# A fused two-model transformer block in fp32 on one core: where the norm factor is applied, which engine adds row sums, and how the decay exponents and the final norm are ordered

## The chip, the cores and the metric

The kernel runs on one core of a Trainium2 chip. TensorE multiplies matrices, VectorE (DVE) and ScalarE (ACT) work on tiles, GpSimd (POOL) does a third share of the elementwise work, and SyncE (SP) issues the DMAs. The metric is the device time of one execution in microseconds; lower is better.

## The reference

The input is 256 tokens of 1024 channels. A first block computes chunked attention, a gated linear recurrence, a merge of the two and a gated feed-forward; its final norm feeds a second block of two layers. Cut to what the change touches:

```python
h = h + (g_a * ya + g_b * yb) @ w_o[l]
hn = rmsnorm(h, norm_ffn_g[l])
g, up = jnp.split(hn @ w_ffn_in[l], 2, axis=-1)
h = h + (jax.nn.silu(g) * up) @ w_ffn_out[l]
return rmsnorm(h, final_norm_g)
...
proj = rmsnorm(h, g) @ w_in                       # gated delta net
qkv = silu(causal_depthwise_conv_2(proj[..., :3 * DN_DIM], conv_w))
gc = cumsum(g); decay = exp(where(tri, gc[:, None] - gc[None, :], -inf))
a_low = where(tri_strict, (k_beta @ k.T) * decay, 0)    # then a triangular solve
...
h = h + square(relu(rmsnorm(h, g) @ w_up)) @ w_down     # mlp, once per layer
return rmsnorm(h, final_norm_g_2)
```

`rmsnorm(x, g)` is x times a factor r of its token (one over the root of the mean square) times g. All of it is float32.

## The kernel before

**Tiling.** The state `H` holds channels on partitions and tokens along the free axis: 8 blocks of 128 channels by 256 tokens. Weights come from HBM in 171 chunks of 128x2048 (1 MB), one at a time through three slots (`RAW`). ScalarE rounds each chunk to fp32r (`WH`, `split_hi`, line 365), VectorE takes the remainder (`WL`, `split_lo`, line 374), and TensorE multiplies in three products: high by high, high by low, low by high (`product`, lines 378 to 380). One chunk makes one step of TensorE: 48 matmuls in `multiply` and `multiply_rows`, 32 in `multiply_wide` (lines 434 and 436). Each step of each engine is written as a body over `st`, and `steps` runs the bodies in a loop of three steps, with a head and a tail unrolled. `split_hi(st)` and `split_lo(st)` work two chunks ahead. All order is written out by hand with semaphores; every engine runs its own program in order.

**Segments**, in order: `xr`, `qk`, `v`, `gr`, `gab`, `ao`, `ro`, `wo`, the feed-forward `fi` (22 chunks) and `fo` (11), then `dq` (12) and `dz` (4), the delta rule without weights, `do`, the first mlp `u0` and `w0` (16 each), `mq`, `mv`, `mo`, the second mlp `u1` and `w1`, and the final norm.

**Norms.** `norm_high` scales two blocks of `H` by the norm's weight and rounds them to `XH` (line 523), and squares them into `XN` (line 516); `norm_low` makes `XL` (line 531). The token's factor r is computed beside the products: POOL adds the squares (`norm_add`), TensorE sums over channels (`norm_sums`), ScalarE takes the root (`norm_root`), VectorE the reciprocal, TensorE turns it into rows (`norm_rows`), and `norm_scale` copies these to `RSTD`. `SUMS_AT` and `ROWS_AT` say after which half step TensorE does its two parts. The output of a projection is multiplied by `RSTD` where it is read out.

**Feed-forward.** In `fi`, ScalarE copies the low half of a step out (`low_half`, line 992), VectorE adds the high half (`add_halves`, line 997), multiplies the gate side by r, and multiplies the two sides after the silu. The up side is not multiplied; r is applied to the output of `fo`. In `u0` and `u1` VectorE computes relu(s) * s (line 1675) on the unscaled s, ScalarE rounds it to `HH` (line 975), VectorE takes `HL` (line 984); r * r is applied to the output of `w0` and `w1`. At the end of `fo`, `w0` and `w1` (`row_chunks`), the last step of TensorE ends one pair of blocks after another. For each pair, VectorE multiplies by `RSTD` into `XN` (`scale_rows`, line 629) and POOL adds that to `H` (`add_rows`, line 642); then ScalarE's `norm_high` and VectorE's `norm_low` prepare the next product, whose first step waits for them pair by pair.

**Delta stage.** During `dq`, VectorE reads each step out into `UQ` (`read_out`, line 1334) and does two taps of the convolution (line 1500); ScalarE does the first tap (line 1163) and POOL the last (`last_tap`, lines 930 and 933). `exponents(g)` builds four heads' decay exponents: two subtractions from rows that TensorE made of `GC` (`decay_rows`), lines 1544 and 1545, and two with `GC` per row, lines 1547 and 1549. `decay_rows(g)` for g of 2 and 3 waits until `exponents(g - 2)` has read its bank. In ScalarE's `dq`, two waits stand ahead of `split_hi`:

```python
if st.i is not None or st.j >= 1:
    act.wait_ge(freed[slot_of(st, -1)], st.uses(-1))
if st.i is not None or st.j >= 3:
    act.wait_ge(s_.tapped, st.local(-3))
split_hi(act, st)
```

**The end.** After `w1` TensorE sums the squares of all 8 blocks over channels with a matrix of ones, so that each partition gets the sum of each token (line 553); ScalarE takes the root of 128x256 (line 574), VectorE the reciprocal of 128x256 (line 1705) and eight products with `H` (line 1709), and SP writes four DMAs.

## Time and profile before

| | us |
|---|---|
| median of 3 runs | 1164.03 (1163.46 to 1165.88) |
| the profiled execution, its own time | 1162.69 |
| its span in the trace | 1161.0 |
| TensorE busy | 1126.1 (97%) |
| VectorE busy | 767.9 (66%) |
| ScalarE busy | 575.7 (50%) |
| POOL busy | 213.3 (18%) |
| mean granted TensorE clock, of full speed | 0.995 |

The span is the time from the first to the last instruction in the trace. A matmul's end is modelled, so neighbouring matmuls overlap in the records; gaps between them are real. "Idle before" is the time in which the engine had nothing to run, with the instruction whose end released it. The chain that ended last is TensorE for 84% of the span and VectorE for 9%.

### The profile page before, as it was taken

What the parts mean: (1) busy time and instruction counts of PE and PEld (TensorE: products, weight loads), DVE (VectorE), ACT (ScalarE), POOL (GpSimd) and SP (SyncE); (2) the same over time, 40 slices, a digit from 0 to 9 for tenths busy, and PEclk for the clock granted to TensorE, in tenths of its full rate; (3) what the DMA queues carried; (4) which work ended last, traced back from release to release, by engine and by line L of the source; (5) the groups of instructions that cost most, each with busy time, mean ns of one, the idle gap of its engine ahead of it and who ended that gap; (6) DMA issues with size and microseconds to landing.
All of it is one profiled execution on the core that took longest, in us unless ns stands there. A gap on an engine that the chain in (4) does not pass through costs nothing.

```text
span 1161.0 us, 21202 instructions
## 1 busy us (share of the span) xinstructions
PE 1126.1 (97%) x8548; PEld 1074.3 (93%) x8548; DVE 767.9 (66%) x944; ACT 575.7 (50%) x749; POOL 213.3 (18%) x222
## 2 busy tenths in 40 slices
PE   6999999999999999998999999999989999999997
PEld 6999889999888999998999888899989999889996
DVE  6647975676877744689896777754467657776333
ACT  6446557445555533565834555543344446554331
POOL 1995003302000001155561010000030002000001
PEclk9999999999999999999999999999999999999999
DMA  9574443645655554345500256655535545655531
GB/s 303 182 232 148 143 138 103 228 158 174 213 186 181 181 210 153 110 146 175 181 8 2 77 178 192 201 188 181 181 115 182 167 140 177 196 186 183 182 142 37
DMA packets 154947, 187.32 MB, mean 161 GB/s; under 512 B 6496, under 2 KB 143872, under 8 KB 154880
## 3 DMA queue, kind: packets, MB, share of 16 engines
q1 hardware_dynamic: 151312, 184.06, 48.5%
q10 hardware_dynamic: 3568, 2.31, 0.7%
q8 instruction: 49, 0.80, 0.3%
q14 instruction: 18, 0.15, 0.0%
HBM read 185.29 MB, written 1.07 MB: 161 GB/s over the span
## 4 chain that ended last, share of the span: by engine, by line
PE 84%; DVE 9%; issue 2%; ACT 2%; DMA 1%; SPq 0%; POOL 0%; DVEq 0%; POOLq 0%; ACTq 0%
PE PS L434 17%; PE PS L378 16%; PE PS L379 16%; PE PS L380 16%; PE PS L436 9%; DVE WL L374 2%; ACT WH L365 1%; DVE XHL L531 1%; PE PS L1892 1%; PE PS L1878 1%; PE PS L723 1%; PE PS L1819 1%; PE PS L1751 1%; DVE QKV L1500 1%; DMA RAW<-in_w_in 1%
## 5 line engine op out<-in xcount | busy, mean ns | idle before, releaser
L374 DVE TENSOR_TENSOR WL<-RAW,WH 128x2048 fp32r<-128x2048 f32 x171 | 405.2, 2370 | 221.5 <-ACT WH L365 221.4
L365 ACT ACTIVATE WH<-RAW 128x2048 fp32r<-128x2048 f32 x171 | 326.8, 1912 | 238.6 <-PE PS L380 196.1
L434 PE MATMUL PS<-XHL,WH 128*128 128x512 f32 x864 | 300.9, 395 | 0.0
L378 PE MATMUL PS<-XHL,WH 128*128 128x256 f32 x832 | 242.5, 291 | 14.9 <-DVE WL L327 6.6
L436 PE MATMUL PS<-XHL,WL 128*128 128x256 f32 x864 | 239.6, 277 | 0.0
L379 PE MATMUL PS<-XHL,WH 128*128 128x256 f32 x832 | 237.1, 285 | 0.0
L380 PE MATMUL PS<-XHL,WL 128*128 128x256 f32 x832 | 236.9, 285 | 0.0
L434 PEld LDWEIGHTS PS<-XHL,WH 128*128 128x128 f32 x864 | 162.1, 188 | 37.5
L378 PE MATMUL PS<-HH,WH 128*128 (+1 forms) x688 | 194.7, 283 | 0.0
L380 PE MATMUL PS<-HH,WL 128*128 (+1 forms) x688 | 194.7, 283 | 0.0
L379 PE MATMUL PS<-HL,WH 128*128 (+1 forms) x688 | 194.7, 283 | 0.0
L378 PEld LDWEIGHTS PS<-XHL,WH 128*128 128x128 f32 x832 | 161.3, 194 | 20.0 <-DVE XHL L531 10.5
L436 PEld LDWEIGHTS PS<-XHL,WL 128*128 128x128 f32 x864 | 162.3, 188 | 0.0
L379 PEld LDWEIGHTS PS<-XHL,WH 128*128 128x128 f32 x832 | 161.3, 194 | 0.3
L380 PEld LDWEIGHTS PS<-XHL,WL 128*128 128x128 f32 x832 | 161.2, 194 | 0.0
L378 PEld LDWEIGHTS PS<-HH,WH 128*128 128x128 f32 x688 | 132.1, 192 | 0.1
L379 PEld LDWEIGHTS PS<-HL,WH 128*128 128x128 f32 x688 | 132.1, 192 | 0.0
L380 PEld LDWEIGHTS PS<-HH,WL 128*128 128x128 f32 x688 | 132.1, 192 | 0.0
L642 POOL TENSOR_TENSOR H<-H,XN 128x512 f32<-128x512 f32 x12 | 15.9, 1328 | 518.7 <-DVE XN L629 518.6
L992 ACT ACTIVATE SG<-PS 128x512 f32<-128x512 f32 x54 | 32.3, 599 | 119.6 <-PE PS L436 119.6
L997 DVE TENSOR_TENSOR SG<-SG,PS 128x512 f32<-128x512 f32 x54 | 37.1, 686 | 55.8 <-ACT SG L992 55.7
L378 PE MATMUL PS<-OH,WH 128*128 128x256 f32 x192 | 54.4, 283 | 0.0
(292 smaller groups left out, 1604.0 us busy)
## 6 DMA issues: line engine op xcount, KB each, us to landing
RAW<-in_mlp_w_up SPq DMA_DIRECT2D x32, 1024.0 KB, 5.4
RAW<-in_mlp_w_down SPq DMA_DIRECT2D x32, 1024.0 KB, 5.0
RAW<-in_w_in SPq DMA_DIRECT2D x26, 1024.0 KB, 5.1
RAW<-in_w_ffn_in_pairs SPq DMA_DIRECT2D x22, 1024.0 KB, 5.1
RAW<-in_dn_w_in SPq DMA_DIRECT2D x16, 1024.0 KB, 5.6
RAW<-in_mb_w_in SPq DMA_DIRECT2D x12, 1024.0 KB, 5.2
RAW<-in_w_ffn_out SPq DMA_DIRECT2D x11, 1024.0 KB, 5.0
RAW<-in_w_attn_out SPq DMA_DIRECT2D x4, 1024.0 KB, 5.2
```

Source lines behind the costliest of these rows:

```text
L365: act.activation(WH[:, k], RAW[:, k], ACT.Copy).then_inc(hi_done, 1)
L374: dve.tensor_tensor(WL[:, k], RAW[:, k], WH[:, k].bitcast(F32), ALU.subtract).then_inc(lo_done, 1)
L378: pe.matmul(out, wh, xh, start=start, stop=False, skip_group_check=True)
L379: pe.matmul(out, wh, xl, start=False, stop=False, skip_group_check=True)
L380: return pe.matmul(out, wl, xh, start=False, stop=stop, skip_group_check=True)
L434: pe.matmul(out.rearrange("p (e t) -> p e t", e=2), h[:, k, part], XHL[:, :, k], start=(k == 0), stop=False, skip_group_check=True)
L436: mm = pe.matmul(out[:, TOK:512], l[:, k, part], XH[:, k], start=False, stop=(k == KB - 1), skip_group_check=True)
L531: ins = dve.scalar_tensor_tensor(out=XL[:, j], in0=H[:, j], scalar=weight(m, j), in1=XH[:, j].bitcast(F32), op0=ALU.mult, op1=ALU.subtract)
L642: ins = pool.tensor_tensor(hb, hb, XN[:, 2 * b:2 * b + 2, :], ALU.add)
L723: mm = pe.transpose(PS[:, 5 + e, P * b:P * b + P], PR[:, e, P * b:P * b + P], IDENT[:])
L992: act.activation(two(SG[:, st.slot]), wide_sides(st)[1], ACT.Copy).then_inc(s_.low_out, 1)
L997: dve.tensor_tensor(two(SG[:, st.slot]), two(SG[:, st.slot]), wide_sides(st)[0], ALU.add).then_inc(freed[st.slot], 1)
```

## The change

- In `fi` both sides are multiplied by r. In `u0` and `u1` VectorE computes relu(s) * r into `SG`, and ScalarE squares it twice, once rounded into `HH` and once into `HP`. The outputs of `fo`, `w0` and `w1` need no factor: VectorE adds them to `H` itself, straight from PSUM. `norm_scale` stands in the first step of `u0` and `u1`, and `ROWS_AT` of their norms is 3, not 5.
- In ScalarE's `dq` the two waits stand behind `split_hi`, ahead of what needs them, and the 12 steps are unrolled.
- `exponents(g)` runs one step later, and its two operations with `GC` are POOL's, after its last tap. `decay_rows(2)` comes after the last step of `dq`, `decay_rows(3)` after the first of `dz`. POOL's two products on all of `H` (lines 945 and 947) come after the copies of the triangular solve.
- The final norm sums by columns: two sums per partition instead of 256, a root and a reciprocal of 128x2, two transposes to rows, and four products of 128x512 with `OUTG` (`H` times the weight, made by ScalarE). POOL adds most of the squares.

```diff
-        ROWS_AT = [4, 3, 2, 5, 3, 5]
+        ROWS_AT = [4, 3, 2, 3, 3, 3]
...
+        def final_scaled(act, p):
+
+            for j in (2 * p, 2 * p + 1):
+                ins = act.activation(OUTG[:, j], H[:, j], ACT.Copy, scale=weight(FINAL, j))
+            ins.then_inc(s_.outg, 1)
...
             if m == FINAL:
-                for j in range(KB):
-                    if j % 2 == 0:
-                        pe.wait_ge(s_.sq_done, 4 * m + j // 2 + 1)
-                    mm = pe.matmul(PS[:, 4, 0:TOK], ONES[:], XN[:, j], start=(j == 0), stop=(j == KB - 1))
+                pe.wait_ge(s_.sq_added, 6)
+                for j in (0, 1, 6, 7):
+                    if j == 6:
+                        pe.wait_ge(s_.sq_done, 4 * m + 4)
+                    for c in range(TT):
+                        mm = pe.matmul(PS[:, 4 + c, 0:P], XN[:, j, c * P:(c + 1) * P], ONES[:], start=(j == 0), stop=(j == 7),
+                                       skip_group_check=True)
...
-        def scale_rows(dve, sg, m):
-
+        def add_rows(dve, sg, m):
 
             for b in range(4):
                 if b < 3:
                     dve.wait_ge(s_.rows_done, 3 * h4_no[sg.name] - 2 + b)
                 else:
                     dve.wait_ge(mm_done, sg.first + sg.n)
-                dve.tensor_tensor(XN[:, 2 * b:2 * b + 2, :], PS[:, b, :].rearrange("p (c t) -> p c t", c=2), by_rows(2),
-                                  ALU.mult).then_inc(s_.rows_scaled, 1)
-                if b > 1 and m != FINAL:
-                    norm_low(dve, m, b - 2)
...
                 hb = H[:, 2 * b:2 * b + 2, :]
-                ins = pool.tensor_tensor(hb, hb, XN[:, 2 * b:2 * b + 2, :], ALU.add)
+                ins = dve.tensor_tensor(hb, hb, PS[:, b, :].rearrange("p (c t) -> p c t", c=2), ALU.add)
...
+                if b and m != FINAL:
+                    norm_low(dve, m, b - 1)
+            if m != FINAL:
+                norm_low(dve, m, 3)
...
+            pool.wait_ge(s_.gc_done, 1)
+            for g in range(4):
+                r = slice(4 * g, 4 * g + 4)
+                by = GC[:, r, None].to_broadcast([P, 4, P])
+                pool.wait_ge(s_.b_read, g + 1)
+                pool.tensor_tensor(AM[:, r], AM[:, r], by, ALU.add).then_inc(s_.dt_ready, 1)
+                pool.tensor_tensor(AT[:, r], AT[:, r], by, ALU.subtract).then_inc(s_.dt_ready, 1)
...
             def dq(st):
-                if st.i is not None or st.j >= 1:
-                    act.wait_ge(freed[slot_of(st, -1)], st.uses(-1))
-                if st.i is not None or st.j >= 3:
-                    act.wait_ge(s_.tapped, st.local(-3))
                 split_hi(act, st)
...
                 if st.i is not None or st.j >= 1:
+                    act.wait_ge(freed[slot_of(st, -1)], st.uses(-1))
                     tap0(st)
                 if st.i is not None or st.j >= 3:
+                    act.wait_ge(s_.tapped, st.local(-3))
                     silu(st)
-            steps(act, seg["dq"], dq, head=3, tail=3)
+            for st in (Step(seg["dq"], j, None) for j in range(seg["dq"].n)):
+                dq(st)
...
+                def square_of(st):
+
+                    k = slot_of(st, -1)
+                    act.wait_ge(s_.sg_in, st.local(base_ - 1))
+                    act.activation(hid(HH, st, 2, 1), two(SG[:, k]), ACT.Square).then_inc(s_.hh_done, 1)
+                    act.wait_ge(s_.hl_done, st.local(base_ - 4))
+                    act.activation(HP[:, k], SG[:, k], ACT.Square).then_inc(s_.hp_done, 1)
...
-                if st.i is None and st.j >= 9:
-                    exponents(st.j - 9)
+                if st.i is None and st.j >= 10:
+                    exponents(st.j - 10)
...
+                    dve.scalar_tensor_tensor(out=two(SG[:, st.slot]), in0=two(SG[:, st.slot]), scalar=0.0, in1=by_rows(2),
+                                             op0=ALU.max, op1=ALU.mult).then_inc(s_.sg_in, 1)
                     if st.i is not None or st.j:
-                        hidden_lo(dve, st, 2, HBASE[f"u{layer}"])
-                    dve.wait_ge(freed[st.slot], st.uses())
-                    dve.scalar_tensor_tensor(out=HP[:, st.slot], in0=SG[:, st.slot], scalar=0.0, in1=SG[:, st.slot],
-                                             op0=ALU.max, op1=ALU.mult).then_inc(s_.hp_done, 1)
+                        square_low(st)
...
-            ch(dve.reciprocal(RSTD[:], RH[:]))
-            ch.wait(dve)
+            dve.reciprocal(RC[:, 0:2], SDC[:, 0:2]).then_inc(s_.rc_ready, 1)
+            dve.wait_ge(s_.rows_ready, FINAL + 1)
             for p in range(4):
-                for j in (2 * p, 2 * p + 1):
-                    ins = dve.scalar_tensor_tensor(out=XN[:, j], in0=H[:, j], scalar=weight(FINAL, j), in1=RSTD[:],
-                                                   op0=ALU.mult, op1=ALU.mult)
-                ins.then_inc(s_.xout, 1)
+                blk = slice(2 * p, 2 * p + 2)
+                dve.wait_ge(s_.outg, p + 1)
+                dve.tensor_tensor(XN[:, blk], OUTG[:, blk], PS[:, 6, None, 0:TOK].to_broadcast([P, 2, TOK]),
+                                  ALU.mult).then_inc(s_.xout, 1)
...
-                if st.i is None and st.j >= 10:
-                    decay_rows(st.j - 8)
+                if st.i is None and st.j == 11:
+                    decay_rows(2)
```

## Rows read from the trace of the kernel before

**Rows 1.** Waits of PE: who waited for whom, us in total, times, longest.
```profile
PE PS L378 <- DVE XHL L531: 5.6, 6, 1.2
PE PS L1784 <- DVE AT L1545: 3.2, 1, 3.2
```
**Rows 2.** Windows: engines' busy us (count), granted PE clock, DMA share, GB/s.
```profile
500.00:510.00 10.00, 8.32 (x68) 8.01 (x68) 9.52 (x10) 6.32 (x9) 4.48 (x3) 1.00 0.36 111
...
540.00:550.00 10.00, 7.28 (x50) 7.28 (x51) 10.00 (x15) 4.85 (x7) 3.70 (x4) 0.83 0.42 127
...
720.00:730.00 10.00, 10.00 (x59) 8.74 (x58) 7.11 (x8) 4.99 (x7) 0.00 (x0) 1.00 0.59 189
```
**Rows 3.** Timeline, end of fo: start, duration, engine, line, [idle before <- releaser].
```profile
459.04 0.69 DVE L629 TENSOR_TENSOR XN<-PS,RSTD 128x512 f32<-128x512 f32 x1 [0.75 <-PE PS L380]
460.48 0.69 DVE L629 TENSOR_TENSOR XN<-PS,RSTD 128x512 f32<-128x512 f32 x1 [0.75 <-PE PS L380]
461.09 1.89 DVE L531 SCALAR_TENSOR_TENSOR XHL<-H,G,XHL 128x256 fp32r<-128x256 f32 x2
...
462.01 0.61 ACT L516 ACTIVATE XN<-H 128x512 f32<-128x512 f32 x1
...
461.32 1.38 POOL L642 TENSOR_TENSOR H<-H,XN 128x512 f32<-128x512 f32 x1 [0.15 <-DVE XN L629]
...
463.13 0.36 PE L378 MATMUL PS<-XHL,WH 128*128 128x256 f32 x1 [1.25 <-DVE XHL L531]
465.45 0.39 PE L378 MATMUL PS<-XHL,WH 128*128 128x256 f32 x1 [0.67 <-DVE XHL L531]
```
**Rows 4.** Timeline, end of w0 and first step of mq.
```profile
856.29 7.05 DVE L531 SCALAR_TENSOR_TENSOR XHL<-H,VEC,XHL 128x256 fp32r<-128x256 f32 x6
863.26 4.48 DVE L374 TENSOR_TENSOR WL<-RAW,WH 128x2048 fp32r<-128x2048 f32 x2
869.51 0.17 DVE L610 RECIPROCAL RC<-SDC 128x2 f32<-128x2 f32 x1 [1.77 <-ACT SDC L576]
...
859.27 3.70 ACT L365 ACTIVATE WH<-RAW 128x2048 fp32r<-128x2048 f32 x2
...
857.86 1.48 POOL L538 TENSOR_TENSOR XN<-XN 128x512 f32<-128x512 f32 x1
...
865.59 0.39 PE L378 MATMUL PS<-XHL,WH 128*128 128x256 f32 x1 [0.51 <-DVE WL L374]
```
**Rows 5.** Timeline of dq, steps 5 to 11.
```profile
502.75 0.38 PE L378 MATMUL PS<-XHL,WH 128*128 128x256 f32 x1 [1.68 <-DVE WL L374]
542.72 1.11 PE L1784 MATMUL PS<-IDENT,GC 128*128 128x128 f32 x4 [3.17 <-DVE AT L1545]
...
511.21 3.41 DVE L374 TENSOR_TENSOR WL<-RAW,WH 128x2048 fp32r<-128x2048 f32 x1 [0.29 <-ACT WH L365]
...
515.48 1.28 ACT L365 ACT_TABLE_LOAD   x1 [2.99 <-DVE UQ L1334]
...
511.18 1.29 POOL L933 TENSOR_TENSOR QKV<-QKV,TAP 128x512 f32 x1 [1.74 <-DVE QKV L1500]
...
535.76 2.29 DVE L374 TENSOR_TENSOR WL<-RAW,WH 128x2048 fp32r<-128x2048 f32 x1 [0.22 <-ACT WH L365]
...
538.57 2.90 DVE L1500 SCALAR_TENSOR_TENSOR QKV<-UQ,VEC,QKV 128x256 f32<-128x256 f32 x4
541.39 0.68 DVE L1544 TENSOR_TENSOR AM<-NEGL,PS 128x512 f32<-128x512 f32 x1
```
**Rows 6.** Timeline of the tail.
```profile
1148.91 0.69 DVE L629 TENSOR_TENSOR XN<-PS,RSTD 128x512 f32<-128x512 f32 x1 [0.75 <-PE PS L380]
1153.34 1.75 DVE L1705 RECIPROCAL RSTD<-RH 128x256 f32<-128x256 f32 x1 [3.74 <-ACT RH L574]
1155.13 3.26 DVE L1709 SCALAR_TENSOR_TENSOR XN<-H,VEC,RSTD 128x256 f32<-128x256 f32 x8
...
1152.84 0.47 ACT L574 ACTIVATE RH<-PS,EPSC 128x256 f32<-128x256 f32 x1 [1.22 <-PE PS L553]
```

More of the change, by code:

```diff
@@ L1153, in row_chunks @@
                     norm_high(act, m, p)
+                    if m == FINAL and p < 3:
+                        final_scaled(act, p)
                 split_hi(act, Step(w, w.n - 1, None))
@@ L1557, in _ @@
                 dve.tensor_tensor(ZS[:, 2 * st.j:2 * st.j + 2], bank(st), by_rows(2), ALU.mult).then_inc(freed[st.slot], 1)
-                if st.j == 0:
-                    exponents(3)
+                if st.j < 2:
+                    exponents(st.j + 2)
             for u in range(2):
@@ L1997, in _ @@
             norm_sums(pe, FINAL)
+            pe.wait_ge(s_.rc_ready, FINAL + 1)
+            for c in range(TT):
+                mm = pe.transpose(PS[:, 6, c * P:(c + 1) * P], RC[:, c:c + 1].to_broadcast([P, P]), IDENT[:])
+            mm.then_inc(s_.rows_ready, 1)
 _VECTORS = [name for name, _ in VECTORS]
```

93 lines of the change are left out of this document (44 added, 49 removed).

## The prediction

> **What bounds the kernel now.** I read the windows of 10 us first. TensorE is busy without a gap in most of them, as in 720 to 730 us, where VectorE has 7.11 and ScalarE 4.99 busy of 10 [rows 2]: there an edit on another engine moves nothing until it passes TensorE. The time to be won is where TensorE's busy time falls short: the ends of `fo` and `w0`, the `dq` stage (8.32 and 7.28 of 10, the latter at a granted clock of 0.83), and the tail. Next I read TensorE's waits. Two of them are what this change is about: `XL` from VectorE, 5.6 us in six waits, and the decay rows, 3.2 us in one [rows 1]. Last, the timeline at each of these places. The reader should see for each gap which instruction ended last, and what that one had waited for. The pitch of a full step follows from the last step of `fo`: VectorE's products at 459.04 and 460.48 each start when 12 matmuls are done, 1.44 us apart [rows 3], so 48 take 5.76 us.
>
> **Row sums, end of `fo`.** Now: VectorE's product (0.69), POOL's addition (1.38), `XH`, then `XL`, and TensorE idles 1.25 and 0.67 us [rows 3]. A pair of `XL` takes 1.89 us with POOL beside it; it can't start in full until POOL ends. After: VectorE adds from PSUM, an operation of the same size as the product, taken at 0.69; `XL` of pair 0 is ready about 460.7, ahead of TensorE's last matmul at about 461.9, and pairs 1 to 3 about 462.4, 464.0 and 465.0, each ahead of the 1.44 us piece that needs it. Both idles go: 1.9 us, and with the restart of the pipe at each about 0.2 us more, say **2.3** (1.7 to 2.4). What is late next, `WL` of `dq`'s second chunk, is covered by the 32 matmuls of the norm sums.
>
> **End of `w0`.** Here POOL goes on with the sums of squares (857.86, 1.48 us) and six `XL` take 7.05 us, more than 1.1 each, where the pair in [rows 3] had 0.95 each. TensorE's second step starts at 865.59, after `WL`, which VectorE could start only at 863.26 though ScalarE had `WH` at 861.2 [rows 4]. After: `H`'s last pair is ready at about 856.7 instead of 857.9, where POOL's additions now end and its squares' begin, ScalarE's `WH` of the second chunk comes about 1.0 earlier, at 860.2, and `WL` may meet one POOL addition (to 861.0) and then takes 2.2: second step at 863.2 instead of 865.6, **2.4**. With no meeting it is 862.4, 3.2; with POOL's additions in turn with each `XL` as now it is 1.0.
>
> On this the Trainium skill (SBUF — State Buffer, "SBUF: two separate sides") says that VectorE with two SBUF inputs and GpSimd take a shared port pair in turn, each for a whole instruction. The 7.05 us agree. By it, the meeting above is certain and 2.4 stands.
>
> **`dq`.** Three things cost TensorE time. (a) Step 5 waits 1.68 us for `WL` [rows 5]: ScalarE's `WH` stood behind its wait for VectorE's read-out and behind a table load. A second table load (515.48, 1.28 us) sits at the loop's second turn, and step 8 is late by about 0.5 for it. (b) From there VectorE has no lead: `WL` with POOL's addition in front of it takes 3.41 instead of 2.29, preceded by 0.29 of waiting for `WH` [rows 5]; the round is about 6.1 against TensorE's 5.76. (c) So `exponents(0)` starts at 541.39 and TensorE stands 3.17 us before decay rows 2, then restarts at 0.83 of its clock over the window, 50 matmuls where about 61 fit in the busy time: another 1.0 us [rows 2, 5].
>
> After: `WH` is early and its table loads go. `WL` then takes the port before POOL's addition; rows of that order are at 535.76: `WL` at 535.76, read-out and taps until 541.39, a round of 5.63 [rows 5]. So step 5 starts on time (1.7, with the restart 1.9), step 8 too (0.6), and VectorE wins about 0.1 a step and 0.8 at the first decay rows, a lead of some 2.6 us at step 11. `exponents(0)` and decay rows 2 both move one step back, so the race is the same one: from `WL` of step 11 VectorE needs two read-outs (0.6 each), two sets of taps (2.8 each), one `WL` (2.2) and 1.2 for the exponents, 10.2 us; TensorE has the lead and one step, 8.4. It waits 1.8 instead of 3.2. A gap of 1.68 us did not lower the clock (1.00 in the window of 500 to 510 [rows 2]), so the 1.0 goes too. Decay rows 3 wait about 0.2 to 0.4. Sum 1.9 + 0.6 + 0.3 (small ones) + 1.4 + 1.0 + 0.3 (no GC operations on VectorE) = **5.5**. Bounds: with rounds of 6.1 as now the lead is gone and the wait is 4.4, the gain 2; with no wait at all it is 7.5.
>
> The eight operations with `GC` go to POOL. No row shows them there; bounds are 0.7 (0.68, VectorE's own at 541.39 [rows 5]) and 1.48 (POOL's addition [rows 4]); I take 1.1, since one operand is a scalar per row. Eight are 9 us, with two or three `WL` in between 14 to 16 us, starting after the last tap at about 557: ready by 573, while TensorE ends `dz` at about 575. The exponentials, a table load (1.28) and the root follow on ScalarE. It is close; I take 0, and up to 2 us of loss. `H`'s two products move behind the solve, where POOL is idle until VectorE's gating: 0.
>
> The Trainium skill (GPSIMD Engine Reference, "3.1 Elementwise — side-by-side cycle accounting") gives a GpSimd addition of two tensors as 1.96 times VectorE's. By that these eight cost 1.34 each, 10.7 us, and end 2 us later, about at the end of `dz`. That speaks against this edit, by up to 1 us.
>
> **Mlp and `fi`.** In `u0` and `u1` VectorE has as many operations as before, one of 128x256 fewer. ScalarE gets one more square of 0.61 [rows 3] a step, about 1.1 in 10 us, to 6.1 of 10. The round across engines is low half, add, relu, two squares, `HL`, but the squares are of the step before. `WH` now comes behind them, about 1.9 us later in the step; `WL` is still 4 us early. In `fi` a product grows from 256 to 512, 0.3 us of VectorE. All this is hidden by TensorE's steps (10.00 busy [rows 2]), cost 0; it costs once VectorE's round passes 5.5 us. Norm rows come a step earlier; the root, the low half, the addition and the reciprocal fit in the half step (2.7 us) before TensorE wants them: 0, at worst 0.5 twice.
>
> **Tail.** Now the last product is at 1148.91, the root at 1152.84 (0.47), the reciprocal 1.75 and eight products 3.26, ending 1158.39 [rows 6]. After: VectorE's addition ends 1149.6, saving POOL's leg. Squares of the last pair end 1150.3; POOL's additions 1150.2; eight matmuls of 128 columns 0.9; root 0.3, bounded by 0.47 above; reciprocal 0.17 [rows 4]; two transposes, less than the 1.11 of four [rows 5], 0.5; and the four products of 512 at 0.6: 1150.3 + 0.9 + 0.3 + 0.2 + 0.5 + 2.5 = 1154.7. Gain **3.7** (3.0 to 4.2). ScalarE's scaled copies lie beside the sums.
>
> **Sum.** 2.3 + 2.4 + 5.5 + 3.7 = 13.9. The profiled execution took 1162.69 with a span of 1161.0, 1.7 around it; it becomes 1147.1 + 1.7 = 1148.8. The median of runs is 1.3 above that execution, so the forecast is 1164.0 - 13.9 = **1150.1**.
>
> **Rivals.** (1) VectorE and POOL keep getting in each other's way in `dq`: rounds stay at 6.1, TensorE waits over 4 us before decay rows 2 and its clock falls to the lower of its levels (1.2 GHz) for a while, as it did after 3.17 us. For it: four of five rounds before were such. Against: the round at 535.76. Gain of `dq` 1.5 to 2: 1154. (2) POOL's eight operations end after `dz`, because each waits for a `WL`: TensorE stands 2 to 4 us before its unit rows and the solve starts late. 1153. (3) Decay rows find `exponents` done, no wait in `dq`, and `XL` meets no POOL: 7.5 + 3.2 instead of 5.5 + 2.4: 1147. (4) Slower: the mlp round. `HL` of a step now waits for ScalarE's second square, and ScalarE's squares wait for VectorE's relu. Should the two go round in one step, serially, the chain is low 0.6, add 0.7, relu 0.7, squares 1.2, `HL` 0.7, `WL` 2.3, 6.2 us with latencies against 5.55, over 32 steps 20 us: 1170. It decides once the chain passes 5.55. Against it: the squares take the tile of the step before, which breaks the ring. (5) The change does not do what it says: the waits at the ends of `fo` and `w0` move to `WH` or `WL` and nothing but the tail comes: 1160.
>
> **Numbers.** The forecast's case (1148.5 to 1151.8) 50%; rival 1 14%, rival 2 11%, rival 3 12%, rival 4 3%, rival 5 3%; 7% for mixtures and what I don't see, some of them slower by one more per cent. The range that leaves out two in ten runs from 1146.0 to 1155.5. Within 0.2% (2.3 us, what a measurement can tell from no change) is 2%, slower by more 4%, faster by more 94%.
>
> **What would show each step.** Right: line 378's waits for `XL` near zero, an addition `H<-H,PS` on VectorE at three ends, `mq`'s second step 8.6 us after its first at most; no wait of a `dq` step for `WL`; decay rows 2 waiting 1 to 2 us at clock 1.00; the tail 5 us from VectorE's last addition to its last product. Wrong: a wait of unit rows for POOL or ScalarE, a granted clock below 1 after `dq`, TensorE below 10.00 of 10 anywhere in `u0` or `u1`.

## The result

The kernel with the change takes 1153.57 us, the median of four runs (1151.71 to 1155.70), against 1164.66 us before in the same set (1163.46 to 1165.88, four runs): a ratio of 0.9905, with a 95% interval of 0.9885 to 0.9926. A later set gave the same kernel 1151.78 (five runs, against 1164.64 before; ratio 0.9894, 0.9873 to 0.9914). So it is faster by 1%, 11.1 us in the one set and 12.9 in the other. The forecast was a gain of 13.9 and a time of 1150.1, which is 3.5 us below the first set's time and 1.7 below the second's. The profiled execution took 1153.67 with a span of 1151.9 us; that of before had 1161.0. The difference of these two traces, 9.1 us, is what is taken apart here; it is less than that of the medians because before's trace is one of its quicker executions (1162.69).

TensorE's waits of the kernel after (who waited for whom, us in total, times, longest):

```profile
PE PS L379 <- DVE WL L375: 2.6, 1, 2.6
...
PE PS L379 <- DVE DOL L1669: 2.0, 1, 2.0
...
PE PS L562 <- POOL XN L976: 1.4, 1, 1.4
PE PS L1798 <- DVE AT L1556: 1.1, 1, 1.1
```

The six waits for `XHL` of [rows 1] are gone, and the wait of the decay rows fell from 3.2 to 1.1 us. The 2.0 us for `DOL`, at the start of `do`, were there before too.

Windows of the kernel after (columns as in [rows 2]; the granted clock is the third number from the right):

```profile
500.00:510.00 10.00, 10.00 (x86) 10.00 (x85) 10.00 (x11) 6.38 (x9) 7.74 (x4) 1.00 0.67 208
540.00:550.00 10.00, 8.90 (x76) 8.70 (x75) 10.00 (x14) 6.11 (x6) 7.01 (x5) 1.00 0.58 195
720.00:730.00 10.00, 10.00 (x60) 8.74 (x59) 7.49 (x7) 5.79 (x8) 0.00 (x0) 1.00 0.58 194
850.00:860.00 10.00, 7.44 (x55) 7.24 (x55) 8.10 (x7) 5.03 (x5) 5.42 (x3) 0.92 0.12 38
...
640.00:650.00 10.00, 7.97 (x55) 7.84 (x54) 6.43 (x9) 4.15 (x6) 0.00 (x0) 0.83 0.23 67
```

`dq` is full now: 10.00 where [rows 2] had 8.32, 8.90 at clock 1.00 where it had 7.28 at 0.83. `u0` is as full as before. But two windows stand below a clock of 1.00 that didn't before: 640 to 650 us, behind the gap at `do`, and 850 to 860, behind the gap in `mq`. (A third such window, 120 to 130 us, lies ahead of all that was changed; it comes below.) The lower level there is 1.2 GHz, half the speed: in 2 us slices `do` reads 0.83 and then 0.50.

End of `fo`, VectorE (start, duration, engine, line):

```profile
460.69 0.69 DVE L636 TENSOR_TENSOR H<-H,PS 128x512 f32<-128x512 f32 x1 [0.75 <-PE PS L381]
461.29 0.87 DVE L538 SCALAR_TENSOR_TENSOR XHL<-H,G,XHL 128x256 fp32r<-128x256 f32 x2
```

Where [rows 3] had a product, an addition of 1.38 on POOL and a pair of `XL` in 1.89, there is one addition of 0.69 and a pair in 0.87, at once.

End of `w0`: POOL, VectorE, TensorE, to be held against [rows 4]:

```profile
853.55 1.28 POOL L549 TENSOR_TENSOR XN<-XN 128x512 f32<-128x512 f32 x1
...
853.76 5.96 DVE L375 TENSOR_TENSOR WL<-RAW,WH 128x2048 fp32r<-128x2048 f32 x2 [1.44 <-ACT WH L366]
...
857.04 0.39 PE L379 MATMUL PS<-XHL,WH 128*128 128x256 f32 x1 [2.56 <-DVE WL L375]
```

The `XL` no longer hold anything up; TensorE waits once, for `WL`, and `WL` waits for POOL's addition, which started 0.2 us ahead of it.

`dq`, steps as in [rows 5], then POOL's operations with `GC`:

```profile
501.89 2.28 DVE L375 TENSOR_TENSOR WL<-RAW,WH 128x2048 fp32r<-128x2048 f32 x1
...
507.50 2.28 DVE L375 TENSOR_TENSOR WL<-RAW,WH 128x2048 fp32r<-128x2048 f32 x1
...
502.26 3.06 POOL L927 TENSOR_TENSOR QKV<-QKV,TAP 128x512 f32 x1 [0.98 <-DVE QKV L1511]
...
542.55 0.65 PE L1798 MATMUL PS<-IDENT,GC 128*128 128x128 f32 x4 [1.10 <-DVE AT L1556]
...
554.41 1.03 POOL L937 TENSOR_TENSOR AM<-AM,GC 128x512 f32<-128x512 f32 x1
555.41 3.09 POOL L938 TENSOR_TENSOR AT<-AT,GC 128x512 f32<-128x512 f32 x1
...
565.50 1.03 POOL L938 TENSOR_TENSOR AT<-AT,GC 128x512 f32<-128x512 f32 x1
```

Two `WL` start 5.61 us apart and take 2.28 each; now it is POOL's addition that stands behind them (3.06 in the place of 1.29).

The tail (VectorE, POOL, TensorE, ScalarE), to be held against [rows 6]:

```profile
1141.87 0.69 DVE L636 TENSOR_TENSOR H<-H,PS 128x512 f32<-128x512 f32 x1 [0.68 <-PE PS L381]
1145.64 0.17 DVE L1719 RECIPROCAL RC<-SDC 128x2 f32<-128x2 f32 x1 [3.08 <-ACT SDC L584]
1146.33 2.48 DVE L1724 TENSOR_TENSOR XN<-OUTG,PS 128x512 f32<-128x512 f32 x4 [0.53 <-PE PS L2016]
...
1141.93 1.27 POOL L976 TENSOR_TENSOR XN<-XN 128x512 f32<-128x512 f32 x1
...
1143.26 2.05 PE L562 MATMUL PS<-ONES,XN 128*128 128x128 f32 x16 [1.43 <-POOL XN L976]
1145.86 0.43 PE L2016 MATMUL PS<-IDENT,RC 128*128 128x128 f32 x2 [0.55 <-DVE RC L1719]
...
1145.35 0.26 ACT L584 ACTIVATE SDC<-PS,EPSC 128x2 f32<-128x2 f32 x1 [2.13 <-PE PS L562]
```

**Where the 9.1 us come from.** I compared the starts of the same event in the two traces. `dq` step 2 starts 2.4 us nearer to `fi` than before (end of `fo`). From there to the unit rows it is 6.7 (`dq`, `dz`). From `u0`'s first matmul to `mq`'s second step it is 2.55 less (1.40 of it at `mq`'s first matmul, 1.15 more at its second step: 9.68 us after the first before, 8.53 after). From the start of VectorE's last row operation to the last product 9.48 became 6.94, and the outputs after it take 3.1 where they took 2.6: 2.06. That makes 13.7. Against it stand 1.5 us twice, for the clock behind `do` and in `mq`, and 1.6 at the very start, in a part that wasn't changed: VectorE's first addition of halves in `fi` is at 288.10 before and at 289.68 after. 13.7 - 3.0 - 1.6 = 9.1. Between `fi` and the tail, before's own trace has one fall of the clock, behind the wait of 3.17 us for the decay rows; that one is gone with the change and is inside the 6.7.

**A measure without the start.** That first addition of `fi` lies between 286.8 and 291.4 us in the fourteen profiles taken here, though no edit touches what runs ahead of it. So below, beside the medians, I give the length from it to the end of the last product, called "length": 870.29 before, 859.13 after, 857.59 for the same kernel unedited in the next set. The 1.5 us between the last two is the clock behind `do`: from its first matmul to `u0` it is 24.60 us in the one and 23.11 in the other.

| kernel | median us (runs) | ratio to before, 95% | length us |
|---|---|---|---|
| unedited, first set | 1153.57 (4) | 0.9905 [0.9885, 0.9926] | 859.13 |
| e1 unedited | 1151.78 (5) | 0.9894 [0.9873, 0.9914] | 857.59 |
| e2 waits first | 1152.00 (4) | 0.9901 [0.9874, 0.9928] | 858.85 |
| e13 waits first, two loads | 1154.36 (4) | 0.9918 [0.9900, 0.9937] | 859.73 |
| e14 two loads | 1153.23 (4) | 0.9910 [0.9893, 0.9927] | 859.40 |
| e3 `GC` on VectorE | 1154.05 (4) | 0.9905 [0.9880, 0.9930] | 859.22 |
| e5 rows by POOL | 1158.80 (4) | 0.9953 [0.9937, 0.9969] | 865.79 |
| e4 old last norm | 1154.21 (4) | 0.9906 [0.9879, 0.9933] | 859.69 |
| e7 tail, 16 columns | 1151.73 (4) | 0.9881 [0.9856, 0.9905] | 858.76 |
| e8 idle matmuls | 1149.36 (4) | 0.9871 [0.9849, 0.9894] | 856.14 |
| e15 e8, one POOL addition | 1149.51 (4) | 0.9870 [0.9850, 0.9889] | 855.54 |
| e16 e15 and seam | 1153.80 (6) | 0.9912 [0.9898, 0.9926] | 859.98 |
| e17 sums in the gap | 1151.17 (5) | 0.9875 [0.9857, 0.9894] | 854.99 |

In the lengths of the unedited kernel's first profile, of e14 and of e7 there is 1.5 us for the clock behind `do`; in the others there is none. The runs come from five sets, each with its own runs of the kernel before, so across sets the ratios and the lengths compare better than the medians.

### The profile page after: what moved, and what is told of

Same layout as the page of the kernel before. It is cut to its first block, busy times and chain, and to the rows that moved or that the text cites. A ratio compares the mean times of both kernels' runs of the same rounds, so it can differ in the third digit from the quotient of the medians.

```text
span 1151.9 us, 21243 instructions
## 1 busy us (share of the span) xinstructions
PE 1124.7 (98%) x8550; PEld 1075.0 (93%) x8550; DVE 766.1 (67%) x930; ACT 588.4 (51%) x786; POOL 222.6 (19%) x220
## 4 chain that ended last, share of the span: by engine, by line
PE 88%; DVE 8%; ACT 2%; DMA 1%; issue 1%; POOLq 0%; POOL 0%; DVEq 0%; SPq 0%; ACTq 0%
PE PS L435 17%; PE PS L379 17%; PE PS L381 17%; PE PS L380 17%; PE PS L437 9%; DVE WL L375 3%; PE PS L1908 1%; PE PS L718 1%; PE PS L1894 1%; DVE QKV L1511 1%; ACT WH L366 1%; DMA RAW<-in_w_in 1%; PE PS L1835 1%; PE PS L668 1%; PE PS L1765 1%
## 5 line engine op out<-in xcount | busy, mean ns | idle before, releaser
L545 POOL TENSOR_TENSOR XN<-XN 128x512 f32<-128x512 f32 x4 | 7.7, 1920 | 362.1 <-ACT XN L517 362.1
```

## Experiments

### The same kernel again: the two gaps and the clock

e1 is the changed kernel with no edit.

> The changed kernel again, unedited. In its trace TensorE idled 2.03 us ahead of do and was then granted 0.83 of its clock over 10 us, where the kernel before idled 2.02 us at the same place and kept 1.00; after the 2.56 us gap ahead of mq's second step it had 0.92 and 0.91. Theory A: what a short gap does to the clock differs from execution to execution. Then this profile differs from the other in at least one of these places, its median is within 1.5 us of 1153.6, and its executions spread by 2 to 4 us, the slower ones at a lower mean clock (1.5 us for each lowered stretch). Theory B: something in the changed kernel lowers the clock at do every time. Then 640 to 650 us shows 0.83 again and the mean clock is 0.994 in every execution. The wait of decay rows 2 is 1.1 us and VectorE's round in dq 5.62 us in either case.

Windows of e1:

```profile
640.00:650.00 10.00, 8.85 (x74) 8.88 (x75) 6.60 (x8) 5.63 (x7) 0.00 (x0) 1.00 0.33 102
850.00:860.00 10.00, 7.44 (x50) 7.24 (x49) 6.05 (x3) 3.39 (x4) 4.90 (x3) 0.83 0.40 131
```

The same gap of 2.0 us ahead of `do` left the clock at 1.00 here and lowered it in the first profile. That is Theory A, but for its median, which came 1.8 below 1153.6 where it allowed 1.5. Of the ten profiles, before's among them, in which that gap stands, three show the clock lowered behind it. The gap in `mq` is 2.56 us, and all eight profiles that have it show the clock lowered. So part of what the edits won in time is given back by the clock in `mq` each time, and behind `do` sometimes. e8 tests that by filling both gaps with matmuls whose result nobody reads:

```diff
@@ tensor engine, ahead of do
+            for _ in range(8):
+                pe.matmul(PS[:, 4, 0:P], IDENT[:], ONES[:], start=True, stop=True)
             steps(pe, seg["do"],
@@ mq, behind its first step
                 norm_point(pe, 4, 2 * t + 1)
+                if t == 0:
+                    for _ in range(10):
+                        pe.matmul(PS[:, 4, 0:P], IDENT[:], ONES[:], start=True, stop=True)
```

> The changed kernel with idle matmuls (128 columns, into a free bank) in two of TensorE's gaps: 8 of them, 1.8 us, ahead of do and 10, 2.2 us, ahead of mq's second step. They end before what TensorE waits for arrives. Theory A: the gaps lower the clock. Then the windows after both show 1.00, the span is up to 3.0 us shorter than the first profile of the changed kernel (1.5 at each), and the executions spread less and have a mean clock of 0.996 or more. Theory B: the clock falls for another reason: 0.83 and 0.92 appear again and the time is the same or up to 0.5 us longer.

Windows of e8:

```profile
640.00:650.00 10.00, 9.76 (x82) 9.63 (x81) 6.60 (x7) 5.36 (x6) 0.00 (x0) 1.00 0.34 107
850.00:860.00 10.00, 9.66 (x83) 9.47 (x82) 6.15 (x3) 4.32 (x4) 4.16 (x3) 1.00 0.48 157
```

Both windows stay at 1.00. From `mq`'s first matmul to VectorE's last row addition it is 291.87 us against 293.34 in e1: 1.47 won, though `mq`'s second step starts no earlier (8.55 us after the first; after: 8.53). The median is 2.4 below e1's, in the same set. The clock in `mq` is shown to be worth 1.5: all eight profiles with the open gap lose it, and the three in which matmuls fill it (e8, e15, e17) don't. For the gap at `do` it is not shown: the clock stayed at 1.00 in all four profiles with that gap filled, but also in seven of the ten with it open. The rest of the 2.4 fits it.

### dq: the waits, the table loads and the order at the port

The change does three things in `dq`: ScalarE's two waits go behind the split, its steps are unrolled (ScalarE loads an activation table 23 times before and 20 times after), and VectorE's operations with `GC` go to POOL. e2 puts the waits back ahead of the split, e13 does that too and brings the table loads back (23 again) by a one-column square root at two steps, e14 has the loads alone.

```diff
             def dq(st):
+                if st.i is not None or st.j >= 1:                            # e2, e13
+                    act.wait_ge(freed[slot_of(st, -1)], st.uses(-1))
+                if st.i is not None or st.j >= 3:
+                    act.wait_ge(s_.tapped, st.local(-3))
+                if st.j in (3, 6):                                           # e13, e14
+                    act.activation(JNK[:], EPSC[:], ACT.Sqrt)
                 split_hi(act, st)
```

> The changed kernel with ScalarE's two waits ahead of split_hi in dq again, the steps still unrolled. Theory A: the place of the waits is what gave VectorE its lead. Then VectorE's WL finds POOL's addition ahead of it again (3.4 us instead of 2.28), its round is 6.0 to 6.1 instead of 5.62, TensorE waits 3.5 to 5 us before decay rows 2 instead of 1.1, perhaps at a lowered clock after it, and the span is 3.5 to 6 us longer. Theory B: the unrolling did it, since it takes ScalarE's table loads out of the loop. Then the round stays near 5.6 and the span changes by less than 1 us.

> As e2 (ScalarE's two waits ahead of the split again, steps unrolled), and ScalarE also runs a one-column square root ahead of the split at steps 3 and 6 of dq, which makes it load a table there and load SiLU's back later: this gives back the two loads that the loop's first turn had. The one-column operation itself is about 0.2 us. Theory A (the two loads made the slow order of the kernel before; each time WH comes 1.3 us late, WL falls behind POOL's addition, and the order then stays): WL 2.6 to 3.4 each with POOL's addition in front, rounds of about 6.0 from step 3 on, decay rows 2 wait 3 to 5 us, the median 3 to 6 us above the unedited one, 1155 to 1158. Theory B (the order heals by itself as it did in e2 after one slow WL): one or two slow WL, rounds of 5.62 again, decay rows 2 wait 2 to 3 us, 1152.5 to 1154.

> The changed kernel with the two waits where the change puts them (behind the split), and with the same two table loads as e13 ahead of the split at steps 3 and 6 of dq. Theory A (with the waits behind the split, ScalarE is ahead by more than a load, so the loads cost nothing): rounds 5.62, decay rows 2 wait 1.1 to 1.3 us, the median as unedited, 1151 to 1153. Theory B (the loads alone are enough to turn the order at the port): rounds of about 6.0, decay rows 2 wait 3 us or more, 1155 to 1157.

From `fi`'s first addition of halves to the unit rows the unedited kernel takes 285.02 us, e2 286.21, e14 285.30, e13 287.10, and before, less the 2.4 at the end of `fo`, 291.7. So the waits alone cost 1.2, the loads alone 0.3, both together 2.1, and together they are more than their sum. In e2 two `WL` are slow (3.12 each) and then they take 2.28 to 2.39 again, with the decay rows waiting 1.7: its Theory A fell, and it cost 0.2 more than Theory B allowed. For e14 Theory A holds in the main: with the waits behind the split the loads cost next to nothing (decay rows wait 1.35). The decay rows of e13 wait 2.1, and TensorE waits another 0.5 for a `WL`. Theory B of e13 holds: after each load the order heals. That isn't what the kernel before did, and the rows show what the difference hangs on. Here is e13 behind its second pair of loads, VectorE, POOL, ScalarE:

```profile
515.24 0.68 DVE L1352 TENSOR_TENSOR UQ<-PS,RSTD 128x512 f32 x1
...
517.90 2.29 DVE L376 TENSOR_TENSOR WL<-RAW,WH 128x2048 fp32r<-128x2048 f32 x1 [0.21 <-ACT WH L367]
...
517.97 3.38 POOL L928 TENSOR_TENSOR QKV<-QKV,TAP 128x512 f32 x1 [1.74 <-DVE QKV L1518]
...
515.95 1.92 ACT L367 ACTIVATE WH<-RAW 128x2048 fp32r<-128x2048 f32 x1 [0.48 <-DVE UQ L1352]
```

and the kernel before in the same place:

```profile
520.94 0.68 DVE L1334 TENSOR_TENSOR UQ<-PS,RSTD 128x512 f32 x1
...
523.69 3.41 DVE L374 TENSOR_TENSOR WL<-RAW,WH 128x2048 fp32r<-128x2048 f32 x1 [0.30 <-ACT WH L365]
...
521.74 1.92 ACT L365 ACTIVATE WH<-RAW 128x2048 fp32r<-128x2048 f32 x1 [0.30 <-DVE UQ L1334]
...
523.66 1.29 POOL L933 TENSOR_TENSOR QKV<-QKV,TAP 128x512 f32 x1 [1.74 <-DVE QKV L1500]
```

and, still before, two steps on, ScalarE and POOL around the `WL` at 535.76 of [rows 5]:

```profile
533.81 1.92 ACT L365 ACTIVATE WH<-RAW 128x2048 fp32r<-128x2048 f32 x1 [2.76 <-DVE UQ L1334]
...
535.81 3.39 POOL L933 TENSOR_TENSOR QKV<-QKV,TAP 128x512 f32 x1 [1.73 <-DVE QKV L1500]
```

In both, `WL` and POOL's addition become ready at almost the same moment, and who starts first has the port. In e13 `WH` starts 0.03 us after the read-out's end (515.92) and `WL` is 0.07 ahead of POOL. Before, `WH` starts 0.12 after it (521.62), and `WL` comes 0.03 behind and lasts 3.41. The remaining difference between the two on ScalarE is that its steps ran in a loop before, and before's own trace ties the 0.09 us to that loop. In the steps inside it that wait for the read-out, `WH` starts 0.12 us after the read-out's end (503.34, 509.26, 521.74 and 527.82); in those of the unrolled steps ahead of it and behind it where it waits for nothing else, 0.03 (478.46, 489.59, 533.81 and 547.66). Three of the loop's `WL` (511.21, 523.69, 529.77) come only 0.03 or 0.04 behind POOL's addition, and in the first unrolled step behind the loop `WL` is 0.05 ahead (535.76 against 535.81) and takes 2.29. So the 0.12 goes with the loop. What the loop costs in all isn't measured: two kernels with it put back (e9 and e10) gave no time.

e3 gives the operations with `GC` back to VectorE:

```diff
-            (POOL: wait gc_done; per group AM += GC, AT -= GC)
+                dve.tensor_tensor(AM[:, r], AM[:, r], per_head(GC[:, r]), ALU.add).then_inc(s_.dt_ready, 1)
+                dve.wait_ge(s_.b_read, g + 1)
+                dve.tensor_tensor(AT[:, r], AT[:, r], per_head(GC[:, r]), ALU.subtract).then_inc(s_.dt_ready, 1)
```

> The changed kernel with the two operations with GC of each exponents(g) on VectorE again instead of POOL. Theory A: they cost VectorE 1.4 to 2.2 us per g while it is late; decay rows 2 still come after the second subtraction and wait 1.1 us, but decay rows 3 come 1.5 to 2 us later and TensorE waits 1 to 2 us for them; span 1 to 2 us longer. Theory B: VectorE has caught up by then and nothing moves (less than 0.5 us). In both, POOL has 8 us less to do in dz.

To the unit rows it takes 286.60, 1.6 more than unedited, and the decay rows wait 2.4 us in two waits (1.1 for decay rows 2, as unedited, and 1.3 for decay rows 3) in the place of 1.1: Theory A. This edit is worth about 1.6.

Of the 6.7 us of this stretch the experiments take back 2.1 (e13) and 1.6 (e3). The clock behind the decay rows (0.83 in [rows 2], 1.00 now) is another 1.5, an estimate from the two falls measured above. About 1.5 are left, and for them the cause is open: no run undoes the loop, nor the later place of `exponents` and `decay_rows`, nor the split that the change also puts ahead of a wait in the first step of `dz`.

### Row sums by POOL again

```diff
-                ins = dve.tensor_tensor(hb, hb, PS[:, b, :].rearrange("p (c t) -> p c t", c=2), ALU.add)
+                dve.tensor_copy(XN[:, 2 * b:2 * b + 2, :], PS[:, b, :].rearrange("p (c t) -> p c t", c=2)).then_inc(s_.rows_scaled, 1)
@@ POOL
+                pool.wait_ge(s_.rows_scaled, 4 * h4_no[sg.name] - 3 + b)
+                ins = pool.tensor_tensor(hb, hb, XN[:, 2 * b:2 * b + 2, :], ALU.add)
```

> The row sums at the ends of fo, w0 and w1 go by the old road: VectorE copies PSUM to XN (a copy in the place of the product with the norm rows), POOL adds XN to H; the norm factor stays in the inner activations and the new last norm stays. Theory A (the ends of fo and w0 are worth what the trace says, 2.4 and 2.5 us, by POOL's leg on the path): TensorE waits for XL again at line 538's tile, 5 to 6 us in six waits; dq's second step 2.4 later, mq's second step 2.4 later, and 0.5 in the tail: 5 us above the unedited kernel, 1156 to 1158. Theory B (the gain came from the norm factor's new place, not from taking POOL out): waits for XL stay near zero and the median within 1.5 us of the unedited, below 1153.5.

Waits of TensorE in e5, then VectorE at the end of `w0` and POOL in the tail:

```profile
PE PS L379 <- DVE XHL L538: 5.6, 6, 1.2
PE PS L562 <- POOL XN L986: 4.8, 1, 4.8
```
```profile
849.00 7.04 DVE L538 SCALAR_TENSOR_TENSOR XHL<-H,VEC,XHL 128x256 fp32r<-128x256 f32 x6
...
1141.00 2.63 POOL L647 TENSOR_TENSOR H<-H,XN 128x512 f32<-128x512 f32 x2
1143.59 1.26 POOL L983 TENSOR_TENSOR XN<-XN 128x512 f32<-128x512 f32 x1
1145.00 1.26 POOL L986 TENSOR_TENSOR XN<-XN 128x512 f32<-128x512 f32 x1
```

The six waits of [rows 1] are back to the tenth of a us, and the six `XL` in 7.04 of [rows 4] too. The end of `fo` costs 2.4 more and that of `w0` 2.5: both terms are shown. The clock in `mq` stays at 1.00 in e5, where the gaps are 1.25 us at most: 1.5 back. The median is 7.0 above e1's and the length 8.2, where Theory A said 5; the miss is the tail, 11.7 us in the place of 6.94. POOL has the row additions first and then the two additions of squares, and TensorE waits 4.8 for them. The new last norm needs POOL free. With it POOL's rows cost 4.8 there; with the old one they cost 0.5 (9.48 before, 9.01 in e4, next).

### The tail

e4 puts the old last norm back (sums as rows, reciprocal of 128x256, eight products); VectorE goes on adding the rows.

```diff
-                pe.wait_ge(s_.sq_added, 6)
-                for j in (0, 1, 6, 7):
+                for j in range(KB):
...
+                    mm = pe.matmul(PS[:, 4, 0:TOK], ONES[:], XN[:, j], start=(j == 0), stop=(j == KB - 1))
...
+            ch(dve.reciprocal(RSTD[:], RH[:]))
...
+                    ins = dve.scalar_tensor_tensor(out=XN[:, j], in0=H[:, j], scalar=weight(FINAL, j), in1=RSTD[:],
+                                                   op0=ALU.mult, op1=ALU.mult)
```

> The changed kernel with the final norm of the kernel before (sums in 8 products of 256 columns, root and reciprocal of 128x256, eight products on VectorE); row sums stay with VectorE. In the first profile of the change VectorE's last product ended 6.3 us after its last row addition; here I add up square 0.63, last two sums 1.1, root 0.47, reciprocal 1.75, products 3.26 and latencies to 7.4. Theory A: the new final norm itself is worth only about 1.1 us, because its sums took 2.05 us instead of the 0.9 that I had forecast, and the rest of the tail's gain came from the row additions. Theory B: it is worth the 3 us of my forecast and something else was lost in the tail.

VectorE in e4:

```profile
1145.42 1.75 DVE L1707 RECIPROCAL RSTD<-RH 128x256 f32<-128x256 f32 x1 [3.27 <-ACT RH L581]
1147.21 3.26 DVE L1711 SCALAR_TENSOR_TENSOR XN<-H,VEC,RSTD 128x256 f32<-128x256 f32 x8
```

From the start of the last row addition to the last product it is 9.01 (before 9.48, after 6.94). With the new norm the same stretch is 2.07 shorter, of which 0.5 goes again at the output. The new norm is worth 1.6 net, nearer to Theory A's 1.1 than to B's 3. The 0.5 goes with the new norm: from the last product to the span's end it is 2.6 us before and in e4 and 3.1 in the other twelve profiles. Why is open.

e7 takes one of POOL's two additions away and makes the sums narrow:

```diff
-                for j in (0, 1, 6, 7):
-                        mm = pe.matmul(PS[:, 4 + c, 0:P], XN[:, j, c * P:(c + 1) * P], ONES[:], ...
+                for j in (0, 1, 4, 5, 6, 7):
+                        mm = pe.matmul(PS[:, 4 + c, 0:16], XN[:, j, c * P:(c + 1) * P], ONES[:, 0:16], ...
```

> The changed kernel with two edits in the final sums: POOL adds only the first two pairs of squares, and TensorE sums the others as they come; and each sum writes 16 columns, not 128. Theory A (the sums' matmuls and POOL's second addition are the tail's next terms): the last square ends 0.1 us after POOL does now, then only four small matmuls follow instead of eight of 0.26 us, so from VectorE's last row addition to its last product it takes 4.7 to 5.0 us instead of 6.25, the span 1.3 to 1.6 us less. Theory B: a matmul costs the load of its 128x128 fp32 block whatever the columns; then four of them take 1 us and it is 5.4 us, 0.8 us less.

TensorE in e7:

```profile
1143.15 2.85 PE L562 MATMUL PS<-ONES,XN 128*128 128x16 f32 x24
```

The 12 matmuls leave 24 records, two each, 0.11 us apart, and 16 columns take what 128 take (e15 has the same 0.11). The tail is 6.59, 0.35 shorter, and both theories had forecast less. The clock falls at its two transposes, which take 0.69 us in the place of 0.43. With 128 columns (e15) the tail is 6.42.

### In search of a better kernel

e15 is e8 with e7's order of sums in columns of 128. e16 is e15 with a seam edit at the end of `w0`: the split of `mq`'s second chunk goes ahead of the fourth pair's high and low halves.

```diff
                 for p in range(4):
+                    if m == 4 and p == 3:
+                        split_hi(act, Step(w, w.n - 1, None))
                     norm_high(act, m, p)
@@ vector engine
+            if m == 4:
+                split_lo(dve, Step(sg, sg.n - 1, None))
             if m != FINAL:
                 norm_low(dve, m, 3)
```

> A candidate for a better kernel, three edits on the changed one: the idle matmuls of e8 (8 ahead of do, 10 ahead of mq's second step); in the tail POOL adds one pair of squares only and TensorE sums blocks 0, 1, 4, 5, 6, 7 in columns of 128; at the end of w0 ScalarE splits mq's second chunk ahead of the fourth pair's high halves, and VectorE its low part ahead of that pair's low halves. Theory A (the gains add): e8's 2.4 us, 0.35 for the tail as in e7, and 0.5 to 1.1 for the seam, since WL is what TensorE waits 2.56 us for there: 1147.7 to 1148.7, ratio about 0.986. Theory B (the seam gives nothing: XL of the fourth pair comes late instead and TensorE stops inside mq's first step): the wait at mq stays within 0.3 us of the old sum of waits, 1149.0 to 1149.5.

> e8 (idle matmuls at both gaps) with one POOL addition in the tail and six blocks summed by TensorE in columns of 128. Theory A (what e16 lost, it lost to the seam edit alone): waits for XL none, clock 1.00 in the windows from 850 to 870, tail 6.6 from the last addition's start to the last XN end, 1148.7 to 1149.4. Theory B (the tail edit is itself a loss, since e7's span was no shorter than the unedited one's): tail 7 or more and 1150 or above.

VectorE and TensorE in e16:

```profile
849.32 2.29 DVE L375 TENSOR_TENSOR WL<-RAW,WH 128x2048 fp32r<-128x2048 f32 x1
851.53 2.89 DVE L538 SCALAR_TENSOR_TENSOR XHL<-H,VEC,XHL 128x256 fp32r<-128x256 f32 x2
...
854.47 0.58 PE L379 MATMUL PS<-XHL,WH 128*128 128x256 f32 x1 [3.44 <-DVE XHL L538]
```

Both theories of e16 were wrong, B by its size. `WL` comes early, but the fourth pair's `XL` stands 2.2 us behind it and then meets POOL's additions (2.89 in the place of 0.88). TensorE stops for 3.44 us inside the first step and the clock falls there: the next records stand 0.21 us apart in the place of 0.12. The ten idle matmuls come behind it, from 857.20 to 859.44, at full speed, but with no gap left to fill, so they are 2.2 us of delay. It costs 4.4 against e15, which has the same tail and idle matmuls, shows none of this (its Theory A) and takes 1149.51, as e8.

e17 attacks POOL's addition instead: POOL adds only two pairs of squares in `mq`, and TensorE sums four blocks in the gap.

```diff
+            if m == 4:
+                pool.tensor_tensor(XN[:, 4:6], XN[:, 4:6], XN[:, 6:8], ALU.add).then_inc(s_.sq_added, 1)
+                return
@@ tensor engine, behind 4 idle matmuls in the place of 10
+            elif m == 4:
+                for c in range(TT):
+                    for j in (0, 1, 4, 5):
+                        mm = pe.matmul(PS[:, 4, c:c + P], XN[:, j, c * P:(c + 1) * P], ONES[:], start=(j == 0), stop=(j == 5))
```

> A candidate: the 8 idle matmuls ahead of do and one POOL addition in the tail as in e16 (no seam edit), and another cure for mq's second step. POOL adds only two pairs of squares there (no third and fourth addition), TensorE sums blocks 0, 1, 4, 5 in eight matmuls, and does them in the gap ahead of the second step, behind four idle ones. Theory A (WL is late there because POOL's third addition, 1.28 us, has the port when WH is ready): WL takes 2.2 to 2.3 us instead of 3.2, TensorE's second step starts 1.0 us earlier than in e8 (852.75 against 853.78 with the same start), two matmuls less stand in the step, the clock stays 1.00; with 0.35 from the tail the time is 1147.5 to 1148.3, about 1.2 to 1.8 below e8. Theory B (WL would take as long without POOL, or the eight matmuls cost more than the gap holds): second step 8.4 us or more after the first, 1149.0 to 1149.6.

VectorE and TensorE in e17:

```profile
853.92 4.49 DVE L375 TENSOR_TENSOR WL<-RAW,WH 128x2048 fp32r<-128x2048 f32 x2 [1.44 <-ACT WH L366]
...
855.39 1.95 PE L578 MATMUL PS<-ONES,XN 128*128 128x128 f32 x16
```

Theory A's mechanism is right: without POOL's last two additions a pair of `WL` takes 4.49 in the place of 5.96, and the first is ready at 856.2. Its price for the matmuls was wrong. A matmul of this type takes 0.23 us (sixteen records for eight), so twelve, the four idle ones among them, last from 854.50 to 857.09 and end 0.9 after `WL`. The second step starts 8.42 after the first, against 7.52 expected. The length is the shortest of all, 854.99, 0.55 below e15, but its five runs (1148.82 to 1151.36) don't show it ahead of e15's four (1148.03 to 1149.81); its profile has a late start (291.37). Which of the two is faster stays open. e8 and e15 have the lowest medians, 2.3 to 2.4 us below e1's (e8 in the same set). Dropping the four idle matmuls of e17 would be the next step; it wasn't tried.

## Why the prediction came out 3.5 us low

The four terms add up to 13.65 in the traces against 13.9 forecast. That close fit is partly luck: `dq` gave 1.2 more than its term and the tail 1.6 less, and the two cancel. What puts the time above the forecast is the granted clock, for which the sum had no term: with both gaps filled (e8) the kernel takes 1149.4, a little under the forecast.

**Row sums, end of `fo`: right.** Forecast 2.3, measured 2.4, and e5 gives 2.4 when it is undone. The waits for `XL` went, and nothing came in their place: `WL` of the second chunk was covered by the norm sums, as said.

**End of `w0`: right in size, short of one consequence.** Forecast 2.4 with one meeting of `WL` and POOL's addition; measured 2.55, with that meeting in the rows (`WL` 3.22 in the place of 2.29), and 2.5 in e5. The prediction asked for the second step at most 8.6 us after the first; it is 8.53. The Trainium skill (SBUF — State Buffer, "SBUF: two separate sides") has the meeting as one of whole instructions; e17 agrees, 4.49 for the pair of `WL` without POOL's additions against 5.96 with them. What the prediction missed is that several short waits became one of 2.56 us. The clock then fell, which cost 1.5 us (e8).

**`dq`: more than forecast, 6.7 against 5.5.** The round was right (5.61 to 5.62 in the trace, 5.63 forecast), and so was the wait of the decay rows, if a bit high (1.10 against 1.8), at clock 1.00. The clock behind the decay rows was priced at 1.0 from a count of matmuls; the falls measured here cost 1.5 each. Of what it put down to `GC` on VectorE, 0.3, e3 measures 1.6: on VectorE these operations stand between the exponents and the next `WL`, at the place where the lead is smallest. Rival 1, rounds of 6.1, didn't come; in three steps of the kernel before the order was decided by 0.03 or 0.04 us at the port. The prediction gave the slow rounds to waits and table loads; they give only 2.1 us (e13), and the loop's 0.09 us a step stood in the trace unread.

**`GC` on POOL: right that it costs nothing, and with more room than feared.** An operation takes 1.03 alone (forecast 1.1). Two met a `WL`, and the last ends at 566.53, about 7 us ahead of the end of `dz`, where 2 were expected. So Rival 2 was far. The Trainium skill (GPSIMD Engine Reference, "3.1 Elementwise — side-by-side cycle accounting") gave 1.34 each, an estimate from its ratio of 1.96 for an addition of two tensors. For additions of two full tensors the trace nearly agrees (1.29 against 0.68, 1.90 times); with one operand a scalar per row it is 1.5 times (1.03 against 0.68), so the page's figure doesn't carry over to that case.

**Mlp and `fi`: right.** 10.00 of 10 with VectorE at 7.49 and ScalarE at 5.79, and a round of 5.55 as before. Rival 4 has nothing for it.

**Tail: the step that was mis-sized, 2.06 against 3.7.** The prediction put eight sums at 0.9. They begin when forecast, 1.39 us after the start of the last row addition, but they leave sixteen records and take 2.05. That is 1.15 of the miss, and the kernel before had it to read, eight matmuls with sixteen records:

```profile
L553 PE MATMUL PS<-XN,ONES x16: 377/379/483, 1148.7 to 1152.4; 128*128 128x256 f32 x16
```

Another 0.5 is lost at the output: the end of the last product came 2.6 ahead of the span's end and now 3.1. The other terms held (root 0.26 for 0.3, reciprocal 0.17, transposes 0.43 for 0.5, products 2.48 for 2.5). From the end of the last addition to the last product it is 6.25, where the prediction's sign was 5.

**What no term held: the clock, 3.0, and the start, 1.6.** The argument was that a gap of 1.68 us had left the clock at 1.00 [rows 2, 5], and that was used for `dq` alone, where it was right. The gap of 2.0 ahead of `do` was there before with clock 1.00, so it was not priced, and nobody can tell from one profile that it falls in some executions and not in others. The gap of 2.56 in `mq` is another matter: the prediction foresaw the step, but not that TensorE would stand idle once for so long, nor asked what that does to the clock. Its own sign of being wrong, "a granted clock below 1 after `dq`", came true. The 1.6 at the start are of the first kind: both traces reach the same wait of 1.89 us at 118.8, and behind it after shows 0.83 in the window of 120 to 130 us and before 1.00. (Earlier it was the other way round, 0.85 before and 1.00 after in the window of 20 to 30, but before started that part sooner and the two were level again at 118.8.)

In sum: 13.9 forecast; +0.1 `fo`, +0.15 `w0`, +1.2 `dq`, -1.6 tail, -3.0 clock, -1.6 start make 9.1.

## What to carry to other kernels

When short waits on the bounding engine are merged into one, look at the granted clock behind it before counting the gain; work that nobody reads, put inside the gap, kept it up in `mq` here, where a fall costs 1.5 us; outside a gap it is pure delay (e16). Where two engines contend for a port, look at which is ready first and by how much: a step that starts 0.1 us later can flip the order for several steps. And price a matmul by the time of a row of the same type, not by the count in the code; a helper engine that enters the tail must also be free there.

## What the hardware showed that was not expected

- The same gap doesn't always do the same to the clock. Behind TensorE's wait of 1.9 us at about 120 us, 7 of 14 profiles show 0.83 in the window and 7 show 1.00, with the same program up to there. Behind 2.0 us ahead of `do` it fell in 3 of 10; behind 2.56 in `mq` in 8 of 8. A fall costs 1.5 us. Ahead of `fi` there are two such gaps, at about 24 us (1.5 to 3.0 us long) and at 119; where the clock fell behind neither, `fi`'s first addition is at 286.8 to 287.9 (four profiles), behind one at 288.1 to 289.7 (six), behind both at 290.8 to 291.4 (four). The spread between runs of one kernel fits this: in the first set the run of 1151.71 has a mean clock of 0.997 and that of 1155.70 has 0.992.
- The order at the shared port keeps itself up. Once `WL` is ahead, POOL's addition waits for it, POOL is late for the next, and `WL` is ahead again (5.62 us a round, e1 and e14). When it is behind, `WL` takes up to 3.41, but that order doesn't last by itself: it turned back after two steps in e2 and in the first step behind the loop in the kernel before. The Trainium skill (SBUF — State Buffer, "SBUF: two separate sides") says that whoever starts first gets the pair for the whole instruction; the trace agrees down to 0.07 us (e13).
- A matmul in full fp32 leaves two records, 0.11 us apart, and takes as long with 16 columns as with 128 (e7 and the unedited kernel); with 256 columns (the sums of the kernel before) the records stand 0.22 apart.
- In the kernel before, ScalarE starts 0.12 us after the end of what it waited for in the steps of a loop, and 0.03 in unrolled steps of the same code.
